# Three norms whose next stage starts on unnormalised chunks, corrected at eviction, and another order for the first norm

## The reference, cut to what matters

```python
def layer_norm(x, g, b):
    mu = jnp.mean(xf, axis=-1, keepdims=True)
    var = jnp.mean(jnp.square(xf - mu), axis=-1, keepdims=True)
    return ((xf - mu) * lax.rsqrt(var + LN_EPS) * g + b)

def squared_relu_mlp(x, w_up, w_down):
    return jnp.square(jax.nn.relu(x @ w_up)) @ w_down

for i in range(2):                       # layer a: dilated attention, layer h: HGRN2
    y = mixer_i(x)
    x = layer_norm(ALPHA * x + y, ln_mix_g[i], ln_mix_b[i])
    y = squared_relu_mlp(x, ffn_w_up[i], ffn_w_down[i])
    x = layer_norm(ALPHA * x + y, ln_ffn_g[i], ln_ffn_b[i])
```

## Time and profile before

| | us |
|---|---|
| runs of the kernel, median (lowest, highest; 3 runs) | 2208.3 (2201.5, 2209.96) |
| the profiled execution, its own time | 2210.26 |
| its span, first to last instruction | 2208.5 |
| PE busy | 2123.1 |
| DVE busy | 1239.5 |
| ACT busy | 898.5 |

### The profile page before, as it was taken

One profiled execution on the slowest core, in us unless ns is written; L12 is line 12 of the kernel. 1 busy time (PEld: TensorE's weight loads), 2 busy tenths in 40 slices (PEclk: granted clock), 3 DMA queues, 4 the chain that ended last, 5 costly groups with the idle time before them and its releaser, 6 DMA issues.

```text
span 2208.5 us, 29665 instructions
## 1 busy us (share of the span) xinstructions
PE 2123.1 (96%) x11082; PEld 1733.5 (78%) x11082; DVE 1239.5 (56%) x2060; ACT 898.5 (41%) x1389; POOL 69.4 (3%) x63
## 2 busy tenths in 40 slices
PE   6999999999999999999999999999999999999997
PEld 5767778888877888888877788888778877888886
DVE  7987544434455666666666642344567676423444
ACT  6244232222236556565552531232255535312322
POOL 1000300000120000000000000000000000000000
PEclk9998999999999999999999999999999999999998
DMA  4102222232232222222221223222111222222221
GB/s 154 38 20 96 95 77 90 87 109 95 84 107 86 87 68 68 86 67 67 86 77 44 77 95 102 92 100 96 69 58 57 95 77 77 95 98 94 97 96 54
DMA packets 31232, 182.96 MB, mean 83 GB/s; under 512 B 5152, under 2 KB 5536, under 8 KB 12448
## 3 DMA queue, kind: packets, MB, share of 16 engines
q1 hardware_dynamic: 28656, 177.95, 23.4%
q10 hardware_dynamic: 1584, 3.71, 0.5%
q0 software_dynamic: 896, 0.06, 0.0%
HBM read 179.54 MB, written 2.10 MB: 82 GB/s over the span
## 4 chain that ended last, share of the span: by engine, by line
PE 88%; DVE 6%; DVEq 2%; ACT 2%; issue 1%; DMA 0%; ACTq 0%
PE ps L585 12%; PE ps L586 12%; PE ps L587 12%; PE ps L1093 6%; PE ps L1095 5%; PE ps L1094 5%; PE ps L1149 3%; PE ps L1151 3%; PE ps L1150 3%; PE ps L1195 2%; PE ps L1197 2%; PE ps L1196 2%; PE ps L646 1%; PE ps L636 1%; PE ps L1004 1%; PE ps L615 1%
## 5 line engine op out<-in xcount | busy, mean ns | idle before, releaser
L1330 ACT ACTIVATE w_hi<-raw 128x2048 fp32r<-128x2048 f32 (+1 forms) x122 | 225.9, 1851 | 298.7 <-PE ps L587 220.2
L585 PE MATMUL ps<-x_hi,w_lo 128*128 128x512 f32 x816 | 317.6, 389 | 0.5 <-DVE y L2264 0.3
L587 PE MATMUL ps<-x_hi,w_hi 128*128 128x512 f32 x816 | 317.5, 389 | 0.0
L586 PE MATMUL ps<-x_lo,w_hi 128*128 128x512 f32 x816 | 317.4, 389 | 0.0
L1784 DVE TENSOR_TENSOR w_lo<-raw,w_hi 128x2048 fp32r<-128x2048 f32 (+3 forms) x116 | 259.2, 2235 | 92.3 <-ACT w_hi L1330 91.5
L1093 PE MATMUL ps<-x_hi,w_lo 128*128 128x512 f32 x544 | 218.9, 402 | 2.9 <-DVE w_lo L2434 2.4
L1095 PE MATMUL ps<-x_hi,w_hi 128*128 128x512 f32 x544 | 213.1, 392 | 0.0
L1094 PE MATMUL ps<-x_lo,w_hi 128*128 128x512 f32 x544 | 212.4, 390 | 0.0
L585 PEld LDWEIGHTS ps<-x_hi,w_lo 128*128 128x128 f32 x816 | 153.2, 188 | 33.1 <-issue 0.7
L587 PEld LDWEIGHTS ps<-x_hi,w_hi 128*128 128x128 f32 x816 | 153.2, 188 | 31.8
L586 PEld LDWEIGHTS ps<-x_lo,w_hi 128*128 128x128 f32 x816 | 153.2, 188 | 31.7
(11 more groups left out here) (463 smaller groups left out, 3923.3 us busy)
## 6 DMA issues: line engine op xcount, KB each, us to landing
raw<-w_attn_in SPq DMA_DIRECT2D x32, 1024.0 KB, 4.9
raw<-w_gate_up SPq DMA_DIRECT2D x22, 1024.0 KB, 4.9
raw<-w_up_a SPq DMA_DIRECT2D x16, 1024.0 KB, 4.9
raw<-w_down_a SPq DMA_DIRECT2D x16, 1024.0 KB, 4.9
raw<-w_up_h SPq DMA_DIRECT2D x16, 1024.0 KB, 4.9
raw<-w_down_h SPq DMA_DIRECT2D x16, 1024.0 KB, 4.9
raw<-w_hgrn_in SPq DMA_DIRECT2D x8, 1024.0 KB, 4.9
raw<-w_down SPq DMA_DIRECT2D x8, 768.0 KB, 4.2
```

The source lines that it names most:

```text
L585: pe.matmul(o, w_lo[:, slot, a:a + P], hi[:, k, :], start=k == 0, stop=False)
L586: pe.matmul(o, w_hi[:, slot, a:a + P], lo[:, k, :], start=False, stop=False)
L587: last = pe.matmul(o, w_hi[:, slot, a:a + P], hi[:, k, :], start=False, stop=k == st.kc - 1)
L1330: act.activation(w_hi[:, slot, 0:width], raw[:, slot, 0:width], ACT.Copy).then_inc(whi_ready, 1)
```

## The change

At the three norms PE runs the first two slabs of the next stage on chunks that are multiplied with the gain but not normalised (`raw_chunk`), between and behind the sums and spreads. ACT makes `raw_hi` beside each square, DVE `raw_lo`. Since the norm is linear in each token, output tile m is then `rstd * (raw - mean * c0) + c1`, where c0 is the product of the weights with the gains and c1 that with the biases. DVE does the first part in place in PSUM, with the sign turned (`correct`, two operations a tile), and ACT adds c1 in the activation that reads the tile anyway. The columns c0 and c1 for 11 output tiles are computed on PE (`fix_tile`: 8 products of 128x128 by 2 columns each), from fp32 weights that POOL's queue loads to `fix_w`. The normalised chunks are still made, for the third slab (`behind_raw`), for head 1, and for the residual. The raw chunks of `mix_a` lie in buffers of their own, those of `ffn_a` and `mix_h` in `x_hi` and `x_lo`, so that ACT there waits for `raw_used` before it overwrites a chunk. In the first norm the squares are made all at once and their sums moved, ACT's 32 angle products stand together, parts of the rotary angles, `d_diag` and the copies of the output matrix go from DVE to ACT, `w_in_tile(5)` moves behind `ssm_in(0)`, and `modulate(0)` ahead of `take(5)`.

```diff
+    FIXES = [("up_a0", 0, 2, 0, "ln_mix_g0"), ("up_a0", 1, 2, 2, "ln_mix_g0"), ("hgrn_in", 0, 2, 4, "ln_ffn_g0"),
+             ("hgrn_in", 1, 1, 6, "ln_ffn_g0"), ("up_h0", 0, 2, 7, "ln_mix_g1"), ("up_h0", 1, 2, 9, "ln_mix_g1")]
...
+            pool.wait_ge(bu_done, BATCHES)
+            for n, (name, c, tiles, col0, g) in enumerate(FIXES):
+                if n >= 2:
+                    pool.wait_ge(fix_done, n - 1)
+                pool.dma_start(fix_w[:, n % 2, 0:tiles * DC * P], w[name][c, :, 0:tiles * DC * P]).then_inc(fix_loaded[n % 2], 16)
...
+            def fix_tile(n, m):
...
+                at_ = 256 + 2 * (col0 + m)
+                for k in range(DC):
+                    a, column = (m * DC + k) * P, GAIN_AT[g] + k
+                    last = pe.matmul(ps[:, 6, at_:at_ + 2], fix_w[:, n % 2, a:a + P], gains[:, column:column + 9:8],
+                                     start=k == 0, stop=k == DC - 1, skip_group_check=True)
...
             ssm_direct(3)
+            pe.wait_ge(pre_gelu, 1)
+            for m in range(2):
+                fix_tile(0, m)
             pe.wait_ge(v_ready, 2)
             ssm_out(2)
             ssm_out(3)
+            for m in range(2):
+                fix_tile(1, m)
...
+                if s % 2 == 0 and s // 2 < len(FIX_TILES):
+                    fix_tile(*FIX_TILES[s // 2])
...
+                raw_chunk(boundary, st, 0, 0)
+                last_sums()
+                raw_chunk(boundary, st, 0, 1)
+                spread_mean()
+                raw_chunk(boundary, st, 0, 2)
                 spread_rstd(var)
+                for k in range(3, DC):
+                    raw_chunk(boundary, st, 0, k)
+                for k in range(DC):
+                    raw_chunk(boundary, st, 1, k)
...
-                dense(f"{up}0", up)
+                behind_raw(f"{up}0", up)
...
+                        if f"{part}_{layer}" in ("ffn_a", "mix_h"):
+                            _, _, used, name, _, tiles = RAW[f"{part}_{layer}"]
+                            if c < DC - 1:
+                                act.wait_ge(raw_used, used + c + 1)
+                            else:
+                                act.wait_ge(tile_done, STAGES[name].tile0 + tiles)
                         act.activation(x_hi[:, c, :], y[:, c, :], ACT.Identity, scale=g, bias=b).then_inc(xhi_ready, 1)
...
+                def beside_chunk(c):
+                    if c in (3, 4):
+                        begun(c - 3)
+                    if c == 4:
+                        split_hi(st, 1, 0)
...
+            def raw_lo(boundary, c):
...
+                stt(lo[:, c, :], y[:, c, :], gain(g, c), hi[:, c, :].bitcast(f32), ALU.mult, ALU.subtract) \
+                    .then_inc(rawlo_ready, 1)
...
+            def correct(boundary, m):
...
+                stt(bank, root[:, :], fix[:, 0, nth:nth + 1], bank, ALU.mult, ALU.subtract)
+                settle()
+                tt(bank, bank, rstd[:, :], ALU.mult).then_inc(corrected, 1)
...
+                def beside_chunk(c):
+                    if c == 2:
+                        correct(f"mix_{layer}", 0)
+                        correct(f"mix_{layer}", 1)
+                    if c == 5:
+                        split_lo(st, 1, 0)
...
+                body(st, 0, 0)
+                correct(f"mix_{layer}", 2)
+                correct(f"mix_{layer}", 3)
+                body(st, 1, 0)
...
-                for g in range(2):
-                    rows, cols = slice(64 * g, 64 * g + 64), slice(16 * g, 16 * g + 16)
-                    tt(ca_re[rows, :, :, cols], ca_part[0][rows], ca_part[1][rows], ALU.subtract)
...
+                tt(ca_part[0][:, :, :, :], ca_part[0][:, :, :, :], ca_part[1][:, :, :, :], ALU.subtract).then_inc(ca_half, 1)
```

More of the change, by code:

```diff
@@ L430, in fold_at, with raw_buffers @@
         return (DC - 1, st.kc - 6 if st.body[0] == 1 else st.kc - 2)
+    def raw_buffers(boundary):
+        if boundary == "mix_a":
+            return hid_hi[:, 8:16, :], hid_lo[:, 8:16, :]
+        return x_hi, x_lo
     def joins(p):
@@ new lines, in behind_raw @@
+            def behind_raw(name, operand):
+                st = STAGES[name]
+                slot = st.slab0 % 2
+                pe.wait_ge(wlo_ready, st.slab0 + 3)
+                for k in range(DC):
+                    pe.wait_ge(xlo_ready, XB[operand] + k + 1)
+                    for m in range(2):
+                        if k == 0:
+                            pe.wait_ge(tile_free["act"], st.free0 + m + 1)
+                        o, a = ps[:, four_banks(st, m), :], (m * DC + k) * P
+                        pe.matmul(o, w_lo[:, slot, a:a + P], x_hi[:, k, :], start=k == 0, stop=False, skip_group_check=True)
+                        pe.matmul(o, w_hi[:, slot, a:a + P], x_lo[:, k, :], start=False, stop=False, skip_group_check=True)
+                        last = pe.matmul(o, w_hi[:, slot, a:a + P], x_hi[:, k, :], start=False, stop=k == DC - 1,
+                                         skip_group_check=True)
+                        if k == DC - 1:
+                            last.then_inc(tile_done, 1)
+                slab(st, 1, 1)
+                with pe.Fori(2, st.trips) as i:
+                    for c in range(len(st.body)):
+                        slab(st, c, i)
@@ L1404, in _ @@
             last.then_inc(kt_ready, 1)
+            for n, (dense_ca, ca) in enumerate(((sq_dense, ca_re), (ca_dense, ca_im))):
+                act.wait_ge(ca_half, n + 1)
+                for g in range(2):
+                    rows, cols = slice(64 * g, 64 * g + 64), slice(16 * g, 16 * g + 16)
+                    last = act.activation(ca[rows, :, :, cols], dense_ca[rows, :, :, :], ACT.Copy)
+            last.then_inc(ca_ready, 1)
             split_hi(w_in, 3, 0)
@@ L2057, in _ @@
             take(0)
+            input_parts(0)
+            input_parts(1)
+            settle()
+            input_matrix()
             take(1)
[L2059 to L2064 removed]
             take(2)
@@ L2534, in body @@
                             dve.sem_inc(folded, 1)
+                        if boundary in RAW and not paired and shift < t < DC - 1:
+                            for d in range(t) if t == shift + 1 else (t - 1,):
+                                raw_lo(boundary, d)
+                        if paired and t == DC - 2:
+                            next_lo(st, 0)
+                            next_lo(st, 1)
+                            raw_lo(boundary, 0)
                 for i in range(st.trips):
@@ L2640, in step @@
                 a, old = hd - 1, 1 - par
-                if project:
-                    split_next(hd, par, 1 if first(hd) else 0)
+                if project and not first(hd):
+                    split_next(hd, par, 0)
                 if attend:
```

363 lines of the change are left out of this document (238 added, 125 removed).

## The result

The changed kernel took 2252.15 us in the median of 4 runs (2250.48 to 2255.64), the kernel before beside it 2209.08 (2201.5 to 2209.96): a ratio of 1.0211, 95% interval [1.0193, 1.023]. It is slower by 43 us, where +22 was forecast.

What follows compares the result with a forecast made beforehand. PE, busy for 96% of the span, plus the few places where it waits was taken as the bound. From the 2208.3 us median, -5 + 11.9 + 0.4 + 2 + 7 + 6 = +22.3 gave 2230.6 us, range 2192 to 2243.

Steps and rivals of the forecast that it cites:

- the correction products: Attention stage: seven tiles at 1.70 us on full PE, +11.9 us, plus 0.4 for copies and waits.
- The first norm: Start of kernel: DVE work freed, less four correction tiles ahead of the first scores; -5 us, between 0 and -8.
- mix_a: First mix norm: raw slabs end earlier, but DVE's order delays third and fourth slab; +2 us, between -7 and +4.
- Rival A: Norms: DVE and ACT less tightly coupled, third slabs ready when PE is; -18 us, 2190 us; chance 0.17.
- mix_h: Second mix norm: ACT's x_hi waits for PE, third slab 3.5 us later than at mix_a; +6 us, between 0 and +8.
- ffn_a: Norm before head 1: ACT and DVE wait for each other, k_dec comes 5.7 us later; +7 us, between -3 and +9.
- Rival B: Attention stage: correction products cost nothing, fitting into time PE spends waiting; +10.4 us, 2219 us; chance 0.10.
- C: Whole kernel: gains at start and norms cancel the tiles' cost within 0.5%; +7 us, 2216 us; chance 0.13.
- D: Correction weights arrive late or PE's order blocks an attention step; +5 to +12 us more, 2240 us; chance 0.10.

Runs made afterwards that it cites:

- wide: The changed kernel with each correction product 64 columns wide in place of two (the same two columns 32 times), results unchanged; 2240.1 us (ratio 1.0153).
- best: reorder, with the norm ffn_a as in the kernel before and the correction products 64 columns wide; 2212.5 us (ratio 1.0033).
- one_product: The changed kernel with one of the eight products of each correction tile, output not the reference's; 2224.1 us (ratio 1.0082).
- start_only: Of the change only the rearranged first norm and first stage; three norms as in the kernel before, no correction products; 2200.66 us (ratio 0.9972).
- no_correct: The changed kernel without DVE's two operations of each correction at the two mix norms, output not the reference's; 2242.6 us (ratio 1.0175).
- reorder: mix_h_own with, at both mix norms, ACT's third-slab split behind chunk 2 and DVE's corrections and split part reordered; 2244.7 us (ratio 1.0173).
- mix_h_own: The changed kernel with the raw chunks of mix_h in buffers that x_hi does not share, no ACT wait on raw_used there; 2248.7 us (ratio 1.02).
- ffn_lag: The changed kernel with DVE's x_lo at ffn_a done for chunk c - 3 behind chunk c, in place of c - 1; 2247.1 us (ratio 1.0191).

## Why the prediction was wrong

**The failed step** is in the part on the correction products: "I take 1.70, since only the column count differs", with the clock left out of the sum for them. The rows last what was taken (1.70), but behind them PE often runs at 1.2 GHz with no wait in front: 17 us of half clock between the tiles of the attention stage, and 6.8 behind the pairs ahead of it. The attention stage is 22.7 us longer where the sum had 12.3 (11.9 + 0.4); 7.6 of the difference are gone in `wide`, and 2.8 us more ahead of the stage. `wide` shows that it is the clock and that the narrow products bring it down: same rows, same length, clock 1.00, 12 us faster. All seven traces with whole narrow tiles have half clock between the tiles, and `wide`, `best` (wide too), `one_product` and `start_only` have none before the stage's token sums. `one_product` shows that nothing else of the correction products (loads, waits) counts. The other 2.8 us of the stage are there in `wide` as well; in `start_only`, which has no tiles, the stage is already 1.7 us longer by the half clock behind those sums. Why narrow products bring the clock down behind some tiles and not behind others stays open.
The row that should have raised the question stood in the forecast itself: the token sums of the norm, of the same narrow form, had a stretch at 0.50 behind them (1226.6 to 1230.2), which I put down to the idle time between. That was a part only: the half clock runs from 1222.3, at the end of sums that PE worked through without a gap, to 1232.5. In the changed kernel there is no idle time between, and the stretch is there all the same (1247.0 to 1250.6, above).
The Trainium skill (TensorE: Matmul & The Clock Gate, "What's actually happening") says that the clock follows how busy PE has been of late; the trace's busy time does not show that, since PE reads 20.00 of 20 us busy at 0.80 and at 0.83.

**The first norm** was taken as -5; what DVE frees is worth 6.6 us at the scores and 9.4 at the glu stage (`start_only`), but with the four tiles in front only 2.0 are left of it: they cost 7.4 us where I let "some 3 us of them show". The wide tiles cost 4.6 there, so 2.8 of the 7.4 are the clock. `scores1` starts 0.5 us earlier (132.92 in the change), not 3 to 5. The hope that the half clock from 133 to 140 would go was right without tiles and wrong with them (clock 0.83 from 120 to 140 in the change). Term -5, measured -2.0; other executions of the same program have -3.8 to +1.9 at this place.

**mix_a** was right in its mechanism and its places to 0.7 us; the term of +2 measured +4.1. Up to the fourth slab it is +2.3, where +1.6 was worked out (1219.4 + 26.2 + 1.4 is 1247.0, not the 1246.3 that I wrote, and the half clock behind the sums delays the raw slabs further); the half clock behind the fourth slab's wait adds the other 1.7 us. I had set one half-clock stretch of before against that. It could not be set so: the half clock of before was already inside the 1264.4 that I compared with. Rival A is out: DVE's order binds as written, which `no_correct` (4.7 us for 5.7 of work) and `reorder` (the order alone 2.4 us here) confirm.

**mix_h**, +6, measured +7.1, and up to +8.8 in other executions of the same program. Its step, that ACT's `x_hi` stands behind PE, is right (`mix_h_own`), but the third slab comes 5.1 us later than at `mix_a`, not 3.5; that the part as a whole changes by 3.5 us is luck. **ffn_a**, +7, measured +9.7; the stall of 5.1 us at the first `x_lo` was 5.09, `k_dec` was ready 6.6 us later where 5.7 was worked out, and the rest stands behind it, where the clock is at half from 1650.0 to 1660.2. Taking the two engines' coupling apart is worth 5.0 us (`ffn_lag`), 3.7 of them by the time that `k_dec` comes.

Rival B (free products) and C are out. D gave a time nearest to the result, 2240, but for a mechanism that did not occur: the weights arrive in time. The range ended at 2243 because no case held a clock that the new products themselves bring down. Over the whole execution the mean granted clock is 0.970 in the change and 0.975 in `wide`: an estimate from these and the spans is 135 us at half clock against 112, worth some 11 us, which is about what the two times differ by.

## What to carry to other kernels

Small products added to a stage in which PE is full can cost twice: their own rows, and what they do to the granted clock behind them; look at the clock behind the nearest narrow rows before pricing them, and widen the products if that costs no time. Work that PE can start before a norm is done only helps if the engines that prepare the next slab are ahead: here DVE was given 14 more operations at a mix norm (8 for `raw_lo`, 8 for the corrections, 2 fewer for `h`) to save PE 7 us of waiting, and the wait came back one slab later. An operand buffer shared between the early and the late form ties three engines together through one semaphore.
